# First units' weights and first tile in halves on two queues, eleven products of ones ahead of them, each gate product one unit later

## The reference, cut to what matters

```python
h = rmsnorm(x, norm_mix_pre[l])
p = h @ w_in
gb, gc, gv, q, k, v, go, lr_f, lr_b = split_cols(p)
y_a = gb * dwconv3(gc * gv, conv_a)
la_f = gate_log_decay(lr_f, gate_up_fwd, gate_bias_fwd)
la_b = gate_log_decay(lr_b, gate_up_bwd, gate_bias_bwd)
...
o_f = gla_chunked(qh, kh, vh, af)
o_b = flip(gla_chunked(flip(qh), flip(kh), flip(vh), flip(ab)))
...
def gate_log_decay(lr, w_up, bias):
    pre = (lr @ w_up + bias).astype(jnp.float32)
    return jax.nn.log_sigmoid(pre) / GATE_NORMALIZER
```

## Time and profile before

| | |
|---|---|
| median of 3 runs | 1728.21 us (1727.53 to 1728.27) |
| profiled execution, its own time | 1729.34 us |
| its span, first to last instruction | 1727.5 us |
| TensorE products busy | 1705.1 us, 99% of the span |
| VectorE, ScalarE, GpSimd busy | 1251.5, 808.3, 355.5 us |
| chain that ended last | 90% TensorE, 5% VectorE, 2% ScalarE |

### The profile page before, as it was taken

The page is one execution under the profiler, slowest core; times in us unless marked ns, Lnnn a source line. Parts: engine busy times, 40 slices in busy tenths (PEclk is TensorE's granted clock), DMA queues, the critical chain, the costliest instruction groups (busy, mean ns, idle before and its releaser), DMA issues.

```text
span 1727.5 us, 21399 instructions
## 1 busy us (share of the span) xinstructions
PE 1705.1 (99%) x8156; PEld 1402.5 (81%) x8156; DVE 1251.5 (72%) x1603; ACT 808.3 (47%) x1090; POOL 355.5 (21%) x155
## 2 busy tenths in 40 slices
PE   7999999999999999999999999999999999999998
PEld 5888888878888788888888888877888888888787
DVE  6564677858899889999887679946476767676534
ACT  5332322245335555555554456423366566666522
POOL 3366565264100000000000000221321211211051
PEclk9999999999999999999999999999999999999999
DMA  5333222135411236555576334412311111102232
GB/s 186 110 110 110 86 86 85 35 119 171 139 64 60 86 107 209 202 177 192 176 257 217 110 109 168 163 55 73 110 43 37 37 38 36 49 22 76 80 134 98
DMA packets 72957, 190.99 MB, mean 111 GB/s; under 512 B 8992, under 2 KB 11424, under 8 KB 72864
## 3 DMA queue, kind: packets, MB, share of 16 engines
q1 hardware_dynamic: 53568, 138.76, 24.5%
q10 hardware_dynamic: 19296, 50.97, 7.9%
HBM read 139.89 MB, written 49.81 MB: 110 GB/s over the span
## 4 chain that ended last, share of the span: by engine, by line
PE 90%; DVE 5%; ACT 2%; issue 1%; DMA 1%; ACTq 0%; DVEq 0%
PE psum L871 21%; PE psum L1175 17%; PE psum L1206 9%; PE psum L910 7%; PE psum L1316 7%; PE psum L1343 5%; PE psum L1063 5%; PE psum L1243 4%; PE psum L1352 4%; PE psum L1332 3%; PE psum L892 1%; PE psum L1268 1%; PE psum L1452 1%; PE psum L924 1%; PE psum L1009 1%
## 5 line engine op out<-in xcount | busy, mean ns | idle before, releaser
L782 POOL TENSOR_TENSOR wl<-wstage,wh 128x1024 fp32r<-128x1024 f32 x64 | 165.4, 2585 | 792.3 <-ACT wh L1479 763.1
L777 POOL TENSOR_TENSOR wh<-wstage,ones 128x1024 fp32r<-128x1024 f32 x43 | 103.1, 2398 | 458.1 <-PE psum L1316 295.6
L871 PE MATMUL psum<-hh,wh 128*128 128x512 f32 x544 | 172.7, 399 | 0.0
L871 PE MATMUL psum<-hl,wh 128*128 128x512 f32 x544 | 167.8, 390 | 0.0
L871 PE MATMUL psum<-hh,wl 128*128 128x512 f32 x544 | 167.6, 389 | 0.0
L2403 DVE SCALAR_TENSOR_TENSOR cc<-uu,col,cc 128x1023 f32<-128x1023 f32 x88 | 113.0, 1284 | 16.8 <-ACT cc L1699 15.2
L2738 DVE TENSOR_TENSOR ptl<-psum,pth 128x512 fp32r<-128x512 f32 x128 | 82.5, 686 | 57.0 <-ACT pth L2006 56.9
L871 PEld LDWEIGHTS psum<-hh,wh 128*128 128x128 f32 x544 | 100.2, 188 | 24.8 <-issue 2.9
L871 PEld LDWEIGHTS psum<-hl,wh 128*128 128x128 f32 x544 | 102.1, 188 | 21.6
L871 PEld LDWEIGHTS psum<-hh,wl 128*128 128x128 f32 x544 | 102.1, 188 | 21.6
L2006 ACT ACTIVATE pth<-psum 128x1024 fp32r<-128x1024 f32 x64 | 65.3, 1021 | 80.4 <-PE psum L1332 80.4
(11 more groups left out here) (428 smaller groups left out, 4440.6 us busy)
## 6 DMA issues: line engine op xcount, KB each, us to landing
wstage<-w_units SPq DMA_DIRECT2D x116, 512.0 KB, 3.6
acts<-cc ACTq DMA_DIRECT2D x22, 512.0 KB, 2.6
yo<-w_units SPq DMA_DIRECT2D x22, 512.0 KB, 7.2
down_sums<-yo SPq DMA_DIRECT2D x22, 512.0 KB, 8.7
wstage<-down_sums SPq DMA_DIRECT2D x44, 256.0 KB, 2.7
wstage<-w_units SPq DMA_DIRECT2D x35, 256.0 KB, 2.9
mix<-spill ACTq DMA_DIRECT2D x12, 512.0 KB, 2.6
kq<-mix SPq DMA_DIRECT2D x16, 256.0 KB, 3.9
```

The source lines that it names most:

```text
L777: pool.tensor_tensor(high, stage(u), ones[:, :].unsqueeze(1).to_broadcast([P, 8, P]), ALU.mult).then_inc(w_high, 1)
L782: pool.tensor_tensor(low, stage(u), high.bitcast(F32), ALU.subtract).then_inc(w_split, 1)
L871: mm = pe.matmul(out[:, t], w[:, wslot, b, :], x[part][:, xk, t], start=start and n == 0, stop=stop and n == 2)
```

## The change

Four edits. (1) SyncE loads the first half (4 blocks) of unit 1, the second half of tile 0's tokens, tiles 1 to 3, the second half of unit 1 and of unit 2 (in two parts), then tiles 4 to 7; ScalarE loads `col`, the first half of tile 0's tokens, and the first half of unit 2. High and low parts of these pieces are made piece by piece, and the squares of a tile come behind the next tile's high part. The new signals are old semaphores under new names (so other places wait for a count that is higher by one or two). (2) `first_units` takes three products of a half of the tokens, then three of the other. (3) GpSimd makes `warm`, ones in float32r, by a multiplication of `ones` with itself, and TensorE runs eleven products of it ahead of the first units; their results are overwritten. (4) Each gate product, and the bias, logs and sums that follow it, come one unit later.

```diff
+        _n, warm = over(("pad20", [P, 8, T], F32), ("warm", [P, 4, P], F32R))
...
+        blocks_in, other_blocks_in, half_in = rope_in, out_done, g_in[1]
+        blocks_high, blocks_low, half_high, half_low = yb_last, mask_set, pad_set, halves_done
...
-            load(1, 1, None)
-            for b in range(0, KT, 4):
-                sync.dma_start(wstage[:, 0, b:b + 4], w_units[dram_unit(2)][:, b:b + 4]).then_inc(w_loaded[0], DMA)
+            def first_blocks(u, blocks, signal):
+
+                sync.dma_start(wstage[:, u % STG, blocks], w_units[dram_unit(u)][:, blocks]).then_inc(signal, DMA)
+
+            first_blocks(1, slice(0, 4), blocks_in)
+            sync.dma_start(xin[:, 0, T1], xT[0][:, T1]).then_inc(half_in, DMA)
+            for k in range(1, 4):
+                sync.dma_start(xin[:, k, :], xT[k]).then_inc(tile_in[k], DMA)
+            first_blocks(1, slice(4, 8), w_loaded[1])
+            for b in (4, 6):
+                first_blocks(2, slice(b, b + 2), w_loaded[0])
...
+            pool.wait_ge(ones_set, 1)
+            each = ones[:, :].unsqueeze(1).to_broadcast([P, 4, P])
+            pool.tensor_tensor(warm[:, :, :], each, each, ALU.mult).then_inc(ones_set, 1)
...
+                def step(u, k, half):
+
+                    t = slice(half * HT, half * HT + HT)
+                    for n, (w, x) in enumerate(((wh, hh), (wl, hh), (wh, hl))):
+                        if (u, n) == (1, 2):
+                            pe.wait_ge(*((half_low, 1) if k == half == 0 else (h_lo, k + 1)))
+                        mm = pe.matmul(slot(u)[:, t], w[:, u, k, :], x[:, k, t], start=k == n == 0,
+                                       stop=k == KT - 1 and n == 2)
+                    return mm
+
                 for k in range(KT):
-                    pe.wait_ge(h_hi, k + 1)
                     for u in (1, 2):
-                        if k == 0:
-                            pe.wait_ge(w_split, u)
-                        for n, (w, x) in enumerate(((wh, hh), (wl, hh), (wh, hl))):
-                            if (u, n) == (1, 2):
-                                pe.wait_ge(h_lo, k + 1)
-                            for half in range(2):
-                                t = slice(half * HT, half * HT + HT)
-                                mm = pe.matmul(slot(u)[:, t], w[:, u, k, :], x[:, k, t], start=k == n == 0,
-                                               stop=k == KT - 1 and n == 2)
+                        if k in (0, 4):
+                            pe.wait_ge(w_split if k else blocks_low, u)
+                        for half in range(2):
+                            if u == 1:
+                                pe.wait_ge(*((half_high, 1) if k == half == 0 else (h_hi, k + 1)))
+                            mm = step(u, k, half)
...
-            pe.wait_ge(ones_set, 1)
+            def warm_up():
+
+                one, wide = warm[:, 0, :], warm[:, :, :]
+                for _n in range(11):
+                    pe.matmul(bank(0), one, wide, start=True, stop=True)
+
+            pe.wait_ge(ones_set, 2)
+            warm_up()
             first_units()
...
-                if u in (3, 5, 7, 9):
-                    gate(u // 2 - 1)
+                if u in (4, 6, 8, 10):
+                    gate(u // 2 - 2)
...
-            for k in range(4):
-                act.dma_start(xin[:, k, :], xT[k]).then_inc(tile_in[k], DMA)
-
-            def high_and_square(src, gain, k, t, used, meanwhile=None):
-
-                act.activation(hh[:, k, t], src, ACT.Copy, scale=col[:, gain + k:gain + k + 1]).then_inc(h_hi, 1)
-                if meanwhile is not None:
-                    weight_high(meanwhile)
+            act.dma_start(xin[:, 0, T0], xT[0][:, T0]).then_inc(tile_in[0], DMA)
+            act.dma_start(wstage[:, 0, 0:4], w_units[dram_unit(2)][:, 0:4]).then_inc(other_blocks_in, DMA)
...
+            def first_high(u, loaded):
+                act.wait_ge(loaded, DMA)
+                act.activation(wh[:, u, 0:4], wstage[:, u % STG, 0:4], ACT.Copy).then_inc(blocks_high, 1)
+
+            def other_high(u):
+                act.wait_ge(*staged(u))
+                act.activation(wh[:, u, 4:8], wstage[:, u % STG, 4:8], ACT.Copy).then_inc(w_act, 1)
...
-            weight_high(1)
+            first_high(1, blocks_in)
             act.wait_ge(col_in, DMA)
-            for k in range(KT):
+            act.wait_ge(tile_in[0], DMA)
+            high(xin[:, 0, T0], C_PRE, 0, T0, half_high)
+            act.wait_ge(half_in, DMA)
+            high(xin[:, 0, T1], C_PRE, 0, T1, h_hi)
+            first_high(2, other_blocks_in)
+            for k in range(1, KT):
                 act.wait_ge(tile_in[k], DMA)
-                high_and_square(xin[:, k, :], C_PRE, k, slice(0, T), 0, None if k else 2)
+                high(xin[:, k, :], C_PRE, k, slice(0, T), h_hi)
+                if k == 3:
+                    other_high(1)
+                    other_high(2)
+                square(xin[:, k - 1, :], k - 1, slice(0, T), 0)
+            square(xin[:, KT - 1, :], KT - 1, slice(0, T), 0)
             weight_high(3)
...
-                if u in (3, 5, 7, 9):
-                    gate_logs(u // 2 - 1)
+                if u in (4, 6, 8, 10):
+                    gate_logs(u // 2 - 2)
...
-            first_low(1)
-            for k in range(KT):
-                low_of(xin[:, k, :], C_PRE, k, slice(0, T), k + 1)
-                if k == 0:
-                    first_low(2)
+            def blocks_of(u, blocks, high_done, signal):
+                dve.wait_ge(*high_done)
+                dve.tensor_tensor(wl[:, u, blocks], wstage[:, u % STG, blocks], f32(wh[:, u, blocks]),
+                                  ALU.subtract).then_inc(signal, 1)
+
+            blocks_of(1, slice(0, 4), (blocks_high, 1), blocks_low)
+            dve.wait_ge(half_high, 1)
+            dve.scalar_tensor_tensor(hl[:, 0, T0], xin[:, 0, T0], col[:, C_PRE:C_PRE + 1], f32(hh[:, 0, T0]),
+                                     ALU.mult, ALU.subtract).then_inc(half_low, 1)
+            low_of(xin[:, 0, T1], C_PRE, 0, T1, 1)
+            blocks_of(2, slice(0, 4), (blocks_high, 2), blocks_low)
+            low_of(xin[:, 1, :], C_PRE, 1, slice(0, T), 2)
+            for k in range(1, KT):
+                if k + 1 < KT:
+                    low_of(xin[:, k + 1, :], C_PRE, k + 1, slice(0, T), k + 2)
+                if k == 2:
+                    blocks_of(1, slice(4, 8), (w_act, 1), w_split)
+                    blocks_of(2, slice(4, 8), (w_act, 2), w_split)
                 if k == 5:
                     first_ranks()
-                if k:
-                    dve.wait_ge(sq_ready, k + 1)
-                    dve.tensor_tensor(root[:, :], root[:, :], sq[:, k % 2, :], ALU.add).then_inc(sq_used, 1)
-                    dve.wait_ge(sq_used, k)
+                dve.wait_ge(sq_ready, k + 1)
+                dve.tensor_tensor(root[:, :], root[:, :], sq[:, k % 2, :], ALU.add).then_inc(sq_used, 1)
+                dve.wait_ge(sq_used, k)
...
-                if u in (3, 5, 7, 9):
-                    biased(u // 2 - 1)
                 if u in (4, 6, 8, 10):
+                    biased(u // 2 - 2)
+                if u in (5, 7, 9, 11):
                     summed_logs(u // 2 - 2)
...
```

More of the change, by code:

```diff
@@ L1089, in next_layer @@
                 for j in range(4):
-                    pe.wait_ge(*((early_low, 2) if n == 2 and j == 0 else (w_split, base + j + 1)))
+                    pe.wait_ge(*((early_low, 3) if n == 2 and j == 0 else (w_split, base + j + 1)))
                     pe.wait_ge(*emptied(2 * j))
@@ L1462, in _, with high, square @@
             act.dma_start(col[:, :], cols).then_inc(col_in, DMA)
-            for k in range(4):
-                act.dma_start(xin[:, k, :], xT[k]).then_inc(tile_in[k], DMA)
-            def high_and_square(src, gain, k, t, used, meanwhile=None):
-                act.activation(hh[:, k, t], src, ACT.Copy, scale=col[:, gain + k:gain + k + 1]).then_inc(h_hi, 1)
-                if meanwhile is not None:
-                    weight_high(meanwhile)
+            act.dma_start(xin[:, 0, T0], xT[0][:, T0]).then_inc(tile_in[0], DMA)
+            act.dma_start(wstage[:, 0, 0:4], w_units[dram_unit(2)][:, 0:4]).then_inc(other_blocks_in, DMA)
+            def high(src, gain, k, t, signal):
+                act.activation(hh[:, k, t], src, ACT.Copy, scale=col[:, gain + k:gain + k + 1]).then_inc(signal, 1)
+            def square(src, k, t, used):
                 if k >= 3:
@@ L1473, in high_and_square @@
                 act.activation(sq[:, k % 2, t] if k else root[:, t], src, ACT.Square).then_inc(sq_ready, 1)
+            def high_and_square(src, gain, k, t, used):
+                high(src, gain, k, t, h_hi)
+                square(src, k, t, used)
+            def first_high(u, loaded):
[4 more added lines that the diff above has]
+                act.activation(wh[:, u, 4:8], wstage[:, u % STG, 4:8], ACT.Copy).then_inc(w_act, 1)
```

(16 more changed lines are left out.)

2 lines of the change are left out of this document (1 added, 1 removed).

## The result

The changed kernel takes 1734.89 us in the median of 5 runs (1734.68 to 1735.18), the kernel before 1728.27 (1727.53 to 1729.04) beside it: a ratio of 1.0038, 95% interval 1.0027 to 1.0049, that is 6.6 us slower. The profiled execution took 1734.68 us with a span of 1732.9; that of before lay 1.1 above its median, so the two traces differ by 5.4 us. The forecast was 1738.0 (1731 to 1742).

A forecast was written before the change was run, and what follows sets the result against it. The prediction took TensorE, busy 1705 of 1727.5 us, to bound the kernel. Its terms, +2.9 (start), +5.5 (hole before the scores) and +1.4 (clock), summed to +9.8: 1728.2 + 9.8 = 1738.0 us, range 1731 to 1742.

The forecast's parts named there:

- rival A: GpSimd's load before the ones is cheap or already done, so the start gains 3.4: 1731.7 us, chance 14%.
- its own sign of being wrong: At the start or scores: TensorE waits for nothing at the first scores, or the first product of ones starts before 3 us.
- The start without its catch: TensorE's first 96 products: halves land earlier, first product about 6.5 us, end 30.1 instead of 33.48, a gain of 3.4.
- The catch, +2.9: GpSimd's MODIFY_POOL_CONFIG load takes 7 us before `warm`, delaying the ones; the 96 products end 2.9 us later, at 36.4.
- The gain of 3.4: TensorE's first 96 products end 3.4 us earlier through halves, if the ones have raised the clock before 6.5.
- The hole, +5.5: TensorE before the first scores: late last gate delays decays, GpSimd's chain and `qi`; scores start at 159.1, not 153.57.
- Rival B: No hole before the scores, as GpSimd and VectorE arrange themselves otherwise, but the load costs: 1731.6 us, chance 9%.
- The clock, half of 2.8 = 1.4: After the idle time before the scores TensorE's clock may drop, costing nothing or 2.8 us; half taken, 1.4.

The follow-up runs named there:

- experiment 11: Changed kernel, gates after units 3, 5, 7, 9, GpSimd splitting unit 4 behind the mask casts, plus a partition_all_reduce before `warm`: 1744.43 us, ratio 1.0090.
- experiment 2: Changed kernel with the gates put back after units 3, 5, 7, 9, so the new start alone: 1734.45 us, ratio 1.0037.
- experiment 8: Changed kernel with gates back after units 3, 5, 7, 9 and GpSimd splitting unit 4 only behind VectorE's mask casts: 1725.65 us, ratio 0.9986.
- Experiments 4 and 5: 4: kernel before, only the last gate one unit later, 1735.00 us; 5: changed kernel, first head's decays ahead of the last gate's logs, 1726.92 us.
- experiment 6: Changed kernel with 22 extra products into an unread bank before TensorE's first wait for `qi`: 1732.99 us, ratio 1.0028.
- experiment 7: Kernel before with only `warm` and the eleven products of ones added: 1728.19 us, ratio 1.0001.

## Why the prediction was right, and where it was wrong

**The sign and the size** held: +6.6 us where +9.8 was forecast, in the range, slower at 0.80. But the sum was right for partly wrong reasons: it is the case called rival A (load free; 1731.7) with a dearer clock and a gain that does not last. The prediction had named its own sign of being wrong, a first product of ones before 3 us, and it came at 2.19. That the time still fell into the range is in part luck: one term 5.0 us too high met another 1.5 us too low.

**The start without its catch: right in its times.** First product 6.75 (6.5), held to 9.55 (9.4), the 96 products end at 30.2 (30.1). Two landings don't follow from the rows given for them: by the earlier trace rows 0.89 MB had moved before 5 us and 1.67 MB by 6.8, not 5.6 and 8. The text put them later without a reason, and the trace bears the later times out (ScalarE's operations on them start at 5.88 and 8.14).

**The catch, +2.9: wrong.** The failed step is "the nearest rows for something fetched ... I take 7 us": the row was taken for a load that must be paid. The trace of before could not price it, and the forecast kept 0 as a lower end but gave it 14%. Measured: 0.1 us in the changed kernel, 9.2 and 9.8 when GpSimd is made to change between two kinds of operation (experiment 11). The order of instructions did hold a hint: GpSimd's rows in the kernel before are memsets and TENSOR_TENSORs, so nothing in the program asks for a change. The Trainium skill, "GPSIMD Engine Reference", section 2.1 Instruction dispatch, speaks of the first call to a freshly loaded kernel, approximately 6 us; the word that mattered is freshly. Experiment 11 measures 9.2 and 9.8, more than the page's figure, while the first loads ran.

**Missing: who else waits for the start.** The gain of 3.4 was carried on as if TensorE were the whole chain. It was 3.2 at unit 3 and 2.1 from unit 4 on: GpSimd began its split of unit 4 at 30.4 instead of 33.6 (the release of its buffer moved with TensorE), onto VectorE's mask casts, and their turns (7.33 against 0.90 alone) ate the earlier start of the reciprocal. The earlier trace rows had shown just this mechanism, and the prediction used it only for the hole. Experiments 2 and 8 show it: with the gates back it costs a wait of 6.4 us, and with GpSimd held back behind the casts all of the 3.2 arrives.

**The hole, +5.5: right**, by its own steps. The `ko` exponent was to end at 141.8 in the time scale of before, which is 139.7 with the 2.1 us gained at the start; it ended at 139.77. Then came `ko`, sum, `ki`, scan, high part, scan, low part and `qi` in turns, 17.1 us from the start of `ko` in the sum and 16.7 in the trace (139.90 to 156.58), and the wait was 5.1. Rival B, that it doesn't open, fell. Experiments 4 and 5 narrow it: the last gate is enough, and only since the decays stand behind its logs on ScalarE. The prediction took "behind them in ScalarE's order" as given; it was the thing to change.

**The clock, half of 2.8 = 1.4: mis-sized.** Measured 2.9 (experiment 6), about the full 2.8 us of the slow stretch of the earlier trace rows. "No idle time between none and 8.66 us is in the trace" was answered by halving; the runs have now 2.0, 5.1 and 6.4 us of idle time, and each was followed by the half pace, while the 0.9 us at 8.6 in the changed kernel was not. The Trainium skill, "TensorE: Matmul & The Clock Gate", Part 1, which the prediction cites, says that an idle array is throttled again. The traces agree with it here: by it the clock's term would have been the full 2.8 us, against 2.9 measured.

In terms of the sum: +2.9 became -2.1 (5.0 too high), +5.5 became +5.1, +1.4 became +2.9 (1.5 too low): +5.9 by the traces at the scores against +9.8.

## What to carry to other kernels

When a change brings one engine forward, list who is released by it: here GpSimd's splits moved with TensorE's buffers and landed on VectorE's casts, and one wait that keeps them apart turned +6.2 us (experiment 2) into -2.9 (experiment 8). A step that is moved later takes with it whatever stands behind it in each engine's order; ask of every one of those whether it needs the moved step, and reorder instead. Products that only raise the clock are worth something only close to the real ones: with 2.0 us between them the clock was down again (experiment 7).

## What the runs showed of the hardware

- VectorE and GpSimd take turns even for small casts: four casts of 128x256 f32 to uint8 took 0.90 us alone, 2.98 beside one GpSimd operation (kernel before) and 7.33 beside three (the changed kernel, from 31.44 us).
- Behind GpSimd's MODIFY_POOL_CONFIG rows the next operation started 0.1 us later in the changed kernel, whose GpSimd runs only MEMSET and TENSOR_TENSOR, and 9.2 and 9.8 us later where it changed to PARTITION_ALL_REDUCE and back, while the first loads ran at 290 to 330 GB/s (the windows 1.2 to 10.5 and 11.8 to 21.7 us of experiment 11).
- 2.0 us of standing still from 6.6 us on, after eleven products, were followed by a granted clock of 0.50 from 9.2 to 12.6 (experiment 7); 0.9 us of it in the changed kernel was not. 5.1 us in the middle of the program cost 2.9 us (experiment 6). Products of ones alone had raised the clock at the start: the first real ones of the changed kernel ran 0.23 us apart (7.78, 8.01, 8.24), those of the kernel before 0.43.
